# A routed-expert kernel: half of the first token tile is found and gathered before the last tile is routed, and the expert weights go through one ring of nine buffers

## What is computed

```
t = h2                                             # 640 tokens x 1024
g = argmax of 4 group logits; two best of that group's 4 expert logits
combine = softmax of the two * probability of the group
for e in range(16):
    he = silu(t @ w1[e]) * (t @ w3[e])             # 1024 -> 512
    y += combine[:, e:e+1] * (he @ w2[e])          # 512 -> 1024
x = x + gate2 * y
```

## Time and profile before

| | us |
|---|---|
| median of 3 runs | 1193.94 |
| lowest and highest | 1192.6, 1195.4 |
| the profiled execution, its own time | 1194.13 |
| its span | 1192.3 |

### The profile page before, as it was taken

One profiled execution on the slowest core, in us unless ns is written; L12 is line 12 of the kernel. 1 busy time (PEld: TensorE's weight loads), 2 busy tenths in 40 slices (PEclk: granted clock), 3 DMA queues, 4 the chain that ended last, 5 costly groups with the idle time before them and its releaser, 6 DMA issues.

```text
span 1192.3 us, 14561 instructions
## 1 busy us (share of the span) xinstructions
PE 1143.1 (96%) x5774; PEld 708.2 (59%) x5775; DVE 534.0 (45%) x1046; ACT 226.1 (19%) x478; POOL 350.4 (29%) x289
## 2 busy tenths in 40 slices
PE   3999999999999999999999999999979999999995
PEld 2666777777777777777777777755543333333432
DVE  3554477454785683384334334535672121211121
ACT  4222366223570002001100010002121011111000
POOL 1585400567003343333333333000011123222222
PEclk9999999999999999999999999999969999999998
DMA  9955020022200222222212225541169999999982
GB/s 353 338 207 202 25 80 4 16 71 80 80 1 1 71 71 72 71 71 71 71 71 71 71 70 217 189 146 66 71 250 404 410 404 413 402 410 405 399 319 29
DMA packets 54005, 201.90 MB, mean 169 GB/s; under 512 B 5360, under 2 KB 5936, under 8 KB 47792
## 3 DMA queue, kind: packets, MB, share of 16 engines
q1 hardware_dynamic: 47056, 185.20, 40.2%
q0 software_dynamic: 6272, 14.17, 4.4%
q10 hardware_dynamic: 608, 1.58, 0.3%
HBM read 189.36 MB, written 18.91 MB: 175 GB/s over the span
## 4 chain that ended last, share of the span: by engine, by line
PE 88%; DMA 9%; DVE 2%; issue 0%; ACT 0%; POOLq 0%; SPq 0%; POOL 0%; DVEq 0%
PE psum L2290 35%; PE psum L2077 12%; PE psum L2354 6%; PE psum L2467 5%; DMA weight_ring<-in_w 4%; PE psum L2198 4%; PE psum L2054 4%; DMA arena<-in_w 3%; PE psum L2258 3%; PE psum L2469 2%; PE psum L2543 2%; PE psum L2491 2%; PE psum L2002 2%; PE psum L2529 2%; PE psum L2232 1%; DMA weight_ring<-in_w_ada 1%
## 5 line engine op out<-in xcount | busy, mean ns | idle before, releaser
L2290 PE MATMUL psum<-arena,weight_ring 128*128 128x320 f32 x928 | 256.9, 432 | 0.0
L2290 PEld LDWEIGHTS psum<-arena,weight_ring 128*128 128x128 f32 x928 | 175.9, 190 | 72.7
L779 POOL TENSOR_TENSOR weight_ring<-weight_ring 128x512 f32<-128x512 f32 x80 | 105.8, 1322 | 347.8 <-DMA weight_ring<-in_w_in 177.0
L2290 PE MATMUL psum<-x,weight_ring 128*128 128x320 f32 x640 | 179.5, 432 | 0.0
L2290 PEld LDWEIGHTS psum<-x,weight_ring 128*128 128x128 f32 x640 | 121.1, 190 | 49.6
L780 POOL TENSOR_TENSOR weight_ring<-weight_ring 128x512 f32<-128x512 f32 x80 | 112.2, 1402 | 0.0
L1562 DVE TENSOR_TENSOR arena<-psum,arena 128x320 f32<-128x320 f32 x124 | 59.5, 488 | 93.1 <-PE psum L2290 92.4
L2077 PE MATMUL psum<-weight_ring,x 128*128 128x256 f32 x384 | 88.0, 380 | 0.0
L2467 PE MATMUL psum<-weight_ring,arena 128*32 128x512 f32 x512 | 77.3, 593 | 3.5 <-DMA weight_ring<-in_w 2.1
L2077 PEld LDWEIGHTS psum<-weight_ring,x 128*128 128x128 f32 x384 | 71.7, 190 | 11.3 <-issue 1.1
L2354 PE MATMUL psum<-weight_ring,arena 128*128 128x512 f32 x160 | 71.8, 596 | 0.0
(11 more groups left out here) (345 smaller groups left out, 1520.9 us busy)
## 6 DMA issues: line engine op xcount, KB each, us to landing
arena<-in_w SPq DMA_DIRECT2D x22, 2048.0 KB, 19.4
weight_ring<-in_w SPq DMA_DIRECT2D x21, 2048.0 KB, 24.9
weight_ring<-in_w_in SPq DMA_DIRECT2D x15, 2048.0 KB, 8.4
arena<-in_w_ada SPq DMA_DIRECT2D x6, 2048.0 KB, 13.1
x<-in_w SPq DMA_DIRECT2D x5, 2048.0 KB, 25.0
x<-in_x_sample SPq DMA_DIRECT2D x2, 2048.0 KB, 12.4
arena<-in_w_ada SPq DMA_DIRECT2D x4, 1024.0 KB, 14.4
weight_ring<-in_w_ada SPq DMA_DIRECT2D x4, 1024.0 KB, 14.3
```

The costliest lines, as they stand in the source:

```text
L779: nc.gpsimd.tensor_tensor(out[:, 0:2], a_[:, 0:2], b_[:, 0:2], op)
L2290: last = mm(product_psum(q, name), w[:, k, :], src[:, k, :], start=(k == 0), stop=(k == 3))
```

## The change

It has four parts.

1. **An early half tile.** The first couple's main tile now holds 64 rows of a and 64 of b (two column groups of 64 instead of four of 32), and they are filled with the first 64 tokens of each expert among the first four token tiles. That is known before the last tile is routed: `first_places` and `first_hots` on DVE make eight one-hot matrices, `first_table` on PE multiplies them, `first_slots`, put into the middle of the last `choose`, writes the list, and GpSimd gathers it. The rest of both experts (32 rows of a, 32 of b) goes to the first half of the shared tile.
2. **PE's order.** The late modulation's parts are spread over the last tile's routing. Then PE waits for the early gather, runs `main_gate(0)`, and only then the tables of all tokens, `main_up(0)`, `weight_table`, the transposes of the second gathered tile and `half_gate_up(0)`. The transpose of the late rows comes after `half_gate_up(0)` instead of before `main_up(0)`.
3. **DVE.** `place_rules` is longer (13 more small instructions) and stands behind the last `choose`. `wide_hots` have five buffers and wait no longer.
4. **One ring.** All 48 loads go through nine buffers of one ring; each load takes the buffer that is freed next, behind one wait for it. Up b of the first couple waits only for four tiles of x to be stored, and its down matrices only for the last residual and for four tiles of h2. The stores of the last tile have semaphores of their own.

`half_down(0)` has three column groups and the first shared tile three adds per output instead of two.

```diff
+def freed_in_order():
+    freed = [(part, which, 0) for part in ("gate", "up") for which in "ab"]
+    for t in range(1, COUPLES - 1):
+        freed += [("gate", "a", t), ("up", "a", t), ("gate", "b", t), ("up", "b", t), ("down", "a", t)]
+        if t == 1:
+            freed.append(("down", "a", 0))
+        if t % 2:
+            freed += [("down", "b", t - 1), ("down", "b", t)]
+    return freed
+HOMES = 9
+LOADS = [name for t in range(COUPLES) for name in matrices(t)]
+HELD_BY = dict(zip(LOADS[HOMES:], freed_in_order()))
...
+def main_lanes(t):
+    return ((0, 64, "a"), (64, P, "b")) if t == 0 else ((0, 32, "a"), (32, 64, "a"), (64, 96, "a"), (96, P, "b"))
+def half_lanes(j):
+    first = ((0, 32, "a", 0), (32, LANE, "b", 0)) if j == 0 else ((0, LANE, "b", 2 * j),)
+    return first + ((LANE, P, "b", 2 * j + 1),)
...
SyncE
+            def last_use(name):
+                part, which, t = name
+                if part == "down":
+                    sp.wait_ge(s_d, 2 * (out_main(t) if which == "a" and t else out_half(t // 2)) + 2)
+                elif which == "b" or t == 0:
+                    sp.wait_ge(s_half_mm, t + 1)
+                else:
+                    sp.wait_ge(s_gate_mm if part == "gate" else s_up_mm, t + 1)
...
+            load("gate", "a", 0, a)
+            job_done(sp, "wo", 2 * NT - 1)
+            load("gate", "b", 0, b)
+            load("up", "a", 0, a)
+            sp.wait_ge(s_outx, 16 * CTX)
+            load("up", "b", 0, b)
+            sp.wait_ge(s_x2, 2 * NT)
+            sp.wait_ge(s_last_scaled, 1)
+            load("down", "a", 0, a)
+            sp.wait_ge(s_h2out, 16 * CTX)
+            load("down", "b", 0, b)
+            sp.wait_ge(s_late, 1)
+            load("gate", "a", 1, a)
+            load("gate", "b", 1, b)
+            sp.wait_ge(s_wtable, NT)
+            load("up", "a", 1, a)
...
GpSimd
             pool.wait_ge(s_slot, 1)
-            pool.wait_ge(s_h2out, 16 * NT)
+            pool.wait_ge(s_h2out, 16 * CTX)
+            gather(0, idxc[:, 1:2], s_xg[0], N_LAT)
+            pool.wait_ge(s_slot, 2)
+            pool.wait_ge(s_last_h2out, 16)
...
-            for n in range(XG):
+            for n in range(1, XG):
                 gather(n, idx[:, TOKEN_TILES[n]:TOKEN_TILES[n] + 1], s_xg[n])
...
VectorE
+            def first_places():
+                second, far, apart, start = part16[0], part16[2], part16[4], part16[5]
+                link(V.tensor_scalar(apart, far, 1.0, float(EMPTY), ALU.is_ge, mult))
+                link(V.scalar_tensor_tensor(out=start, in0=second, scalar=float(EARLY_ROWS), in1=apart, op0=mult, op1=add))
+                early = masks[:, 0:CTX].rearrange("p i j e -> p (i j) e")
+                link(V.tensor_tensor(first_looked, early, start.unsqueeze(1).to_broadcast([P, 2 * CTX, EXPERTS]), mult))
+                V.tensor_scalar(first_past, rank[:, 0:2 * CTX], float(EARLY_ROWS), float(EMPTY), ALU.is_ge, mult)
+                link(V.reduce_sum(first_at, first_looked, axis=AX))
+                link(V.tensor_tensor(first_at, first_at, rank[:, 0:2 * CTX], add))
+                link(V.tensor_tensor(first_at, first_at, first_past, add))
+            def first_hots():
+                for h in range(2):
+                    part = slice(CTX * h, CTX * (h + 1))
+                    V.tensor_tensor(first_hot[:, part, :], first_at[:, part].unsqueeze(2).to_broadcast([P, CTX, SLOTS]),
+                                    ramp[:, 0:SLOTS].unsqueeze(1).to_broadcast([P, CTX, SLOTS]), ALU.is_equal).then_inc(s_hot, 1)
+            def first_slots():
+                dve.wait_ge(s_table, 1)
+                link(V.tensor_scalar(idxc[:, 0:1], first_psum, float(EMPTY), None, add))
+                V.tensor_scalar(idxc[:, 1:2], idxc[:, 0:1], EMPTY - 1, None, ALU.bitwise_and).then_inc(s_slot, 1)
...
             x2_sum(NT - 1)
-            place_rules()
+            first_places()
             x2_rstd(NT - 1)
             dve.sem_inc(s_last_rstd, 1)
-            choose(NT - 1)
+            first_hots()
+            choose(NT - 1, first_slots)
             dve.wait_ge(s_last_scaled, 1)
             h2_shifted(NT - 1)
+            place_rules()
             rules_found()
...
TensorE
+            def first_table():
+                for n in range(2 * CTX):
+                    if n % CTX == 0:
+                        pe.wait_ge(s_hot, n // CTX + 1)
+                    last = mm(first_psum, first_hot[:, n, :], pair_vals[:, n // 2:n // 2 + 1], start=(n == 0), stop=(n == 2 * CTX - 1))
+                last.then_inc(s_table, 1)
             route_part(NT - 1, ps, 0)
-            x2_T(2 * NT - 1)
-            route_part(NT - 1, ps, 1).then_inc(s_job, 1)
             ada_part(LAST_PAIR, late_psum, range(0, 1), late_slot)
+            x2_T(2 * NT - 1)
+            ada_part(LAST_PAIR, late_psum, range(1, 2), late_slot)
+            route_part(NT - 1, ps, 1).then_inc(s_job, 1)
+            ada_part(LAST_PAIR, late_psum, range(2, 3), late_slot)
+            first_table()
+            ada_part(LAST_PAIR, late_psum, range(3, ADA_STEPS), late_slot).then_inc(s_late, 1)
             rank(NT - 1)
             count(NT)
...
+            next_tokens(0)
+            main_gate(0)
+            for i in range(NT):
+                table(i)
+            pe.wait_ge(s_late_rows, 1)
+            pick_lanes(late_T_psum, late_rows).then_inc(s_lateT, 1)
+            main_up(0)
             pe.wait_ge(s_order, 1)
             weight_table(range(NT))
-            next_tokens(0)
-            main_gate(0)
-            pe.wait_ge(s_late_rows, 1)
-            pick_lanes(late_T_psum, late_rows).then_inc(s_lateT, 1)
...
             next_tokens(1)
+            emptied(pe, INDEX[("rank", NT - 1)])
+            half_gate_up(0)
             pe.wait_ge(s_late_mod, 1)
             tr(late_rows_psum[0:16, 0:P], rowpack[:, 48:64], ident[:, :]).then_inc(s_late_packT, 1)
-            main_up(0)
-            half_gate_up(0)
             hidden_T(0)
             next_tokens(2)
```

More of the change, by code:

```diff
@@ L207, in job_bank @@
 def job_bank(j):
+    if JOBS[j][:2] == ("rank", NT - 1):
+        return 4
     if JOBS[j][:2] in START_BANK:
@@ L279, in down_count, with matrices @@
-def down_count(which, t):
-    name = (which, t)
-    return sum(DOWN_UNIT[n] == DOWN_UNIT[name] for n in DOWN_LOADS[:DOWN_LOADS.index(name) + 1])
+def matrices(t):
+    a, b = ("b", "a") if t + 1 == COUPLES else ("a", "b")
+    return [(part, which, t) for part in ("gate", "up", "down") for which in (a, b)]
+def freed_in_order():
[7 more added lines that the diff above has]
+    return freed
@@ L293, in build @@
+def half_lanes(j):
+    first = ((0, 32, "a", 0), (32, LANE, "b", 0)) if j == 0 else ((0, LANE, "b", 2 * j),)
+    return first + ((LANE, P, "b", 2 * j + 1),)
+EARLY_ROWS, LATE_ROWS = 64, 32
+ADDS = sum(2 if t < WHOLE else 1 for t in range(COUPLES)) + sum(len(half_lanes(j)) for j in range(QUADS))
 def build(nc, io):
@@ L473, in build @@
         s_x = sem("x_loaded")
[L474 to L475 removed]
+        s_kc, s_vc = sem("cached_k_loaded"), sem("cached_v_loaded")
         s_w = [sem(f"weights_loaded{s}") for s in range(W_SLOTS)]
@@ L735, in more @@
+            load("gate", "a", 1, a)
+            load("gate", "b", 1, b)
+            sp.wait_ge(s_wtable, NT)
+            load("up", "a", 1, a)
+            load("up", "b", 1, b)
+            load("down", "a", 1, a)
+            load("down", "b", 1, b)
+            for t in range(2, COUPLES):
+                a, b = expert_at(COUPLES - 1 - t), expert_at(COUPLES + t)
+                for part, which, _ in matrices(t):
+                    load(part, which, t, a if which == "a" else b)
             def more(r, c, k):
@@ L1687, in tile_upto, with choose @@
                 return rt[i][:, 48:64]
-            def choose(i):
+            def choose(i, between=None):
                 v = int(i == CTX)
@@ L1705, in choose @@
                 for j, m in enumerate((m1, m2)):
+                    if j and between is not None:
+                        between()
                     link(V.reduce_max(m, score, axis=AX))
@@ L2464, in main_part @@
                     if t < WHOLE:
-                        for lane in range(4):
-                            rows_ = slice(32 * lane, 32 * (lane + 1))
-                            last = mm(out[rows_, :], xgT[:, k, rows_], (b if lane == 3 else a)[:, k, :], start=(k == 0), stop=(k == KT - 1))
+                        for lo, hi, which in main_lanes(t):
+                            last = mm(out[lo:hi, :], xgT[:, k, lo:hi], (b if which == "b" else a)[:, k, :], start=(k == 0), stop=(k == KT - 1))
                     else:
@@ L2488, in half_gate_up @@
                 lo, up, gate = half_base(t), half_base(t), LANE - half_base(t)
+                if t == 0:
+                    gate_a, up_a = weights("gate", "a", t), weights("up", "a", t)
+                    for k in range(KT):
```

(13 more changed lines are left out.)

245 lines of the change are left out of this document (100 added, 145 removed).

## The result

| kernel | median, us | runs | ratio to before (95%) |
| --- | --- | --- | --- |
| before | 1194.02 | 4, 1192.6 to 1195.4 | 1 |
| after | 1204.03 | 4, 1203.3 to 1206.54 | 1.0085 (1.0072 to 1.0097) |

The change costs 10.0 us; 1194.6 was forecast, and at the most 1200.5. The profiled execution of after took 1206.54 us, 2.5 above its own median, with a span of 1204.7; that of before took 1194.13. So the two traces differ by 12.4 us where the medians differ by 10.0. The mean granted clock of the profiled execution of after was also the lowest of its four: 0.983, against 0.985 (1204.57 us), 0.988 and 0.987 (1203.49 and 1203.3).

A forecast was written before the change was run, and what follows sets the result against it. The chain was 88% PE and 9% DMA, with both limits nearly equal in the expert stage. PE's arrival -0.3 plus 1 for ties gave +0.7 on 1194.13, 1194.8, or 1194.6 for the median; range 1189 to 1200.5.

The forecast's parts named there:

- The extra column group and the wider first lanes cost PE nothing: column groups run side by side: In the first couple's main and half tiles, three groups take the same step as before; costed at 0 us.
- The ties: Late rows, adds, hidden(1) and later gathers finish about when PE wants them; 1 us together, ends 0 and 5.
- the late rows and the adds: Slower rival: their delay makes PE wait at hidden_T(1) or later tiles' transposes; five us, 1199, chance 0.22.
- x: How much later the first half_gate_up starts than 916.45; forecast +4.0 us, at 920.4.
- gather, issue to landing: Early gather under the running weight stream, before main_gate(0): 11.3 us, ends 5.0 and 13.8.
- clock in main_gate(0): Half clock after PE's wait for the early gather costs 2.5 us, ends 0 and 3.5.
- Before, PE worked ... at half clock before it rose: In the old kernel, 885.3 to about 892: seven us at half clock worth 3.5; 2.5 taken for the new order.
- the 10.3 worked out from the packets: Early gather's landing time in us if DMA engines alternate unequal packets between queues; would lower the sum by 1.0 us.
- the head start: main_gate(0) starts 5.9 us earlier, at 894.0; less than the 9.8 us added before half_gate_up(0).
- the second gather not waited for: Before half_gate_up(0): lands at 917.7, PE comes at 918.2, so hidden by half a microsecond.
- the pause of the stream: Weight loads pause for two or three us, around 917 to 925, before buffers are freed.
- -0.3: At the last couple's half tile, PE decides and arrives at 1142.2 instead of 1142.5, before the 1 us for ties.

The follow-up runs named there:

- the groups mended: The changed kernel with half_down(0) in four column groups of 32 rows instead of 32, 32 and 64: 1202.17 us, ratio 1.0061.
- the ring with eight products: Kernel before plus one nine-buffer ring, gathers issued before late rows and adds, eight dense filler products, no early tile: 1197.56 us, ratio 1.0023.
- the gathers ahead: GpSimd's gathers issued before the late rows' return and adds: 1202.98 us on the changed kernel, 1196.24 with half_down(0) also in four groups of 32.

## Why the prediction was wrong

**The step that failed: "The extra column group and the wider first lanes cost PE nothing: column groups run side by side".** It was costed at nothing from the pattern of the kernel before, where all groups of a tile have the same width. Three groups of 32, 32 and 64 rows took 15.88 us instead of 7.02, in after and in before alike; four of 32 rows took 7.0. In these runs groups ran side by side only at one width. The Trainium skill (TensorEngine Tiling (Array Packing), "Key Properties") says that a change of the tiling mode, not just of the tile, drains TensorE. The trace agrees: no overlap between the widths (15.88 against 7.02, of which 1.6 us go away when they alternate less). The diff had the third group in plain sight, and this was the rule to weigh. The wider lanes by themselves did cost nothing (7.09 for 32 products of 64 rows).

**The ties were under-sized.** "I put 1 us for the ties together, ends 0 and 5": with the groups mended PE waited 8.2 us for later gathers. Two near ties, before 960, were worked out, and the later gathers behind the adds were not; 7.8 of the 8.2 us lie there. The rival "the late rows and the adds" named the place rightly and gave 5. The return of the late rows took 18.3 us from 938.3, and began 4 us later than forecast, mostly since `half_gate_up(0)` did; the first add began at 961.55, not 957.3. GpSimd's timeline in after:

```profile
938.34 1.14 POOL L907 DMA_DIRECT2D arena<-rows_scratch  x2 [28.19 <-DMA rows_scratch<-arena]
...
961.55 1.47 POOL L889 DMA_INDIRECT y_sample<-arena,slot_rows  x1 [19.51 <-DVE arena L1984]
```

In after these waits don't show, because PE came late to the same places by `half_down(0)`.

**x was 8.1 instead of 4.0.** Of the 4.1 us of error 1.1 is no part of the change as far as the traces show: in the profiled execution of after DVE is that much late before anything that the diff touches on PE (`residual`'s product at 870.76 against 869.70 in before). Over the fourteen traces the same product starts anywhere from 869.58 to 870.98, and at 870.79 in one that has neither the early tile nor DVE's new order (the ring with eight products), so the scatter of single executions is enough to give it. Term by term:

```
term                              forecast   measured
first_hots                             1.3      1.29
gather issued                        879.5      880.2 (879.2 without the 1.1)
gather, issue to landing              11.3      11.9
main_gate(0) starts                  894.0      895.3
clock in main_gate(0)                  2.5       2.4
tables                                 2.2       2.3
weight_table                           4.1       3.3
main_up(0) and pick_lanes              0         3.2
```

The terms from `main_gate(0)` on add up to 3.7 of the 4.1 us. The last line is the largest: "Before, PE worked ... at half clock before it rose" was counted once. In this execution the clock rose in `main_gate(0)` and fell again behind the tables that the change put after it; `main_up(0)` took 9.56 us, where such products take 7.0 at full clock, and `pick_lanes` 1.66 instead of 0.98. Other executions in the same order lost nothing there, and with 922.00 x would be 5.6, 1.6 over the forecast. The value of 11.3 for a gather under the stream was 0.6 too low and the 10.3 worked out from the packets 1.6; the variants' 12.5 to 13.0 lie further off.

**What was right:** when the early list is there; half clock ahead of `main_gate(0)`; the head start, smaller than what was put between; the second gather not waited for; the end of all waits for weights; and the pause of the stream. The last, in stretches of after (columns as above):

```profile
920.00:925.00 5.00, 3.84 (x36) 3.16 (x38) 2.85 (x15) 1.51 (x2) 0.00 (x0) 1.00 0.53 165
...
930.00:935.00 5.00, 4.24 (x35) 2.53 (x29) 0.74 (x1) 2.71 (x5) 0.00 (x0) 1.00 0.49 147
```

The DMA share is 0.53 and 0.49, and 0.65 in between: the share that is missing from 15 us adds up to 6.7 us of pause, where 2 to 3 were forecast, and no wait came of it, since PE itself was late.

**The sum again, with what the runs showed:** -0.3, +4.1 for what x had too little, +8.9 for `half_down(0)` and nothing for the ties, which lie beside it, is 12.7 on the profiled execution of before, where 12.4 was measured. With x at 5.6 it is 10.2, where the medians differ by 10.0. So the width of the groups is nearly all of the error between the medians. With one width in `half_down(0)` x and the ties add instead.

What stays open: why the clock fell behind the tables in three traces and not in four others with the same order there (the fall cost 3.2 us in the profiled execution of after, which fits its being 2.5 above its median); and the wait of 2.0 to 2.6 us for DVE at L2599 in three kernels with the gathers ahead, which fits adds issued later but was not tried by itself. Not tried either: the gathers ahead, or dense products through the wait, in the kernel before with its two rings. So the runs don't say how much of the 4.4 to 4.7 us needs the early tile and the one ring.

## What to carry to other kernels

Column groups of one tile overlapped here only where all had the same width: split a wide group rather than mix widths, even if it means more products. Before you call a stage bound by one thing, list each parallel chain and its slack: here two costs of about eight us hid one another, and mended alone one gave 2 us and the other nothing clear. When work is reordered around a wait, ask what the clock will be after it: put the light products into the wait and the dense ones together behind it, and hold back a full weight stream for a transfer that everything waits for; with the groups mended and the gathers ahead, either ended 4.4 to 4.7 us below the kernel before.

## What the runs showed of the hardware that was not expected

- Column groups of 32 and of 64 in turn: 15.88 us for 48 products, 14.27 with the widths kept apart, 7.0 for 64 products in four groups of 32 or 32 in two groups of 64.
- In after the granted clock fell from 1.00 to 0.50 between 904 and 910 with PE busy for 2.00 of each 2 us, on the 20 tables and `pick_lanes`; in four other traces with the same order there it stayed up. With eight dense products of 512 columns through the wait `main_gate(0)` took 7.09 instead of 9.52 us.
- A gather of 0.52 MB took 11.9 to 13.0 us under the weight stream, 7.9 with SP's next loads held back, 5.0 on idle engines.
